# State-space heads: the decay rows go through device memory and are copied into all partitions, instead of being spread by a product

## The reference

```python
dt = softplus(dt_raw + dt_bias)              # (tokens, 2 directions, 32 heads)
a = -exp(a_log)
y_fwd = _ssd_scan(xs * dt[:, :, 0], dt[:, :, 0] * a[0], bm, cm)
y_bwd = flip(_ssd_scan(flip(xs * dt[:, :, 1]), flip(dt[:, :, 1] * a[1]), flip(bm), flip(cm)))
y = (y_fwd + y_bwd + d_skip * xs) * silu(z)
```

## Time and profile before

| what | value |
|---|---|
| median of 3 runs | 2443.31 us (2442.24 to 2443.97) |
| the profiled execution, its time | 2443.01 us |
| its span, from the first to the last instruction | 2441.1 us |
| PE busy | 2391.5 us (98%) |
| DVE busy | 1713.4 us (70%) |
| ACT busy | 1339.5 us (55%) |
| DMA engines, weight queue | 48.0% of 16 engines |
| granted clock of PE, mean of the span | 0.994 |

### The profile page before, as it was taken

The page is one execution under the profiler, slowest core; times in us unless marked ns, Lnnn a source line. Parts: engine busy times, 40 slices in busy tenths (PEclk is TensorE's granted clock), DMA queues, the critical chain, the costliest instruction groups (busy, mean ns, idle before and its releaser), DMA issues.

```text
span 2441.1 us, 48177 instructions
## 1 busy us (share of the span) xinstructions
PE 2391.5 (98%) x18842; PEld 2289.4 (94%) x18842; DVE 1713.4 (70%) x2517; ACT 1339.5 (55%) x2355; POOL 90.2 (4%) x101
## 2 busy tenths in 40 slices
PE   9999999999999999999999999999999999999998
PEld 8898999999899999999999997899999999789998
DVE  7788777777888867786766575676566657667665
ACT  6788655644678855563444445554444444555443
POOL 0000000000100000000100010010001001001000
PEclk9999999999999999999999999999999999999999
DMA  7454555455354455545455553345545544434553
GB/s 216 131 159 126 165 164 161 154 170 189 108 153 139 137 156 160 169 155 181 145 181 174 169 160 106 121 144 178 170 147 179 178 163 152 123 124 142 189 181 113
DMA packets 401046, 380.19 MB, mean 156 GB/s; under 512 B 28223, under 2 KB 397037, under 8 KB 400765
## 3 DMA queue, kind: packets, MB, share of 16 engines
q1 hardware_dynamic: 397821, 373.87, 48.0%
q10 hardware_dynamic: 3072, 4.20, 0.7%
HBM read 372.77 MB, written 1.05 MB: 153 GB/s over the span
## 4 chain that ended last, share of the span: by engine, by line
PE 79%; DVE 12%; ACT 3%; DVEq 3%; issue 1%; SPq 1%; DMA 1%; ACTq 0%
PE ps L583 22%; PE ps L585 21%; PE ps L584 21%; DVE scratch L1806 3%; DVE w_lo L1583 3%; DVEq L1805 2%; PE ps L805 2%; PE ps L836 1%; PE ps L837 1%; PE ps L838 1%; ACT scratch L1082 1%; ACT w_hi L1082 1%; PE ps L854 1%; PE ps L612 1%; PE ps L614 1%
## 5 line engine op out<-in xcount | busy, mean ns | idle before, releaser
L1583 DVE TENSOR_TENSOR w_lo<-raw,w_hi 128x1024 fp32r<-128x1024 f32 x664 | 812.0, 1229 | 423.2 <-ACT w_hi L1082 421.8
L583 PE MATMUL ps<-x_hi,w_hi 128*128 128x256 f32 (+1 forms) x3664 | 1056.4, 288 | 4.3 <-DVE w_lo L1583 1.6
L584 PE MATMUL ps<-x_lo,w_hi 128*128 128x256 f32 (+1 forms) x3664 | 1042.6, 285 | 0.0
L585 PE MATMUL ps<-x_hi,w_lo 128*128 128x256 f32 (+1 forms) x3664 | 1039.8, 284 | 0.0
L1082 ACT ACTIVATE w_hi<-raw 128x1024 fp32r<-128x1024 f32 x664 | 697.7, 1056 | 447.5 <-PE ps L585 370.6
L583 PEld LDWEIGHTS ps<-x_hi,w_hi 128*128 128x128 f32 x3664 | 690.8, 189 | 30.8 <-issue 25.3
L584 PEld LDWEIGHTS ps<-x_lo,w_hi 128*128 128x128 f32 x3664 | 692.2, 189 | 2.0
L585 PEld LDWEIGHTS ps<-x_hi,w_lo 128*128 128x128 f32 x3664 | 693.6, 189 | 0.0
L583 PE MATMUL ps<-big_r,w_hi 128*128 128x272 f32 (+1 forms) x832 | 238.9, 287 | 0.0
L585 PE MATMUL ps<-big_r,w_lo 128*128 128x272 f32 (+1 forms) x832 | 238.2, 286 | 0.0
L1082 ACT ACTIVATE scratch<-ps 128x256 f32<-128x256 f32 (+9 forms) x328 | 122.3, 384 | 154.9 <-PE ps L838 63.8
(11 more groups left out here) (302 smaller groups left out, 3063.1 us busy)
## 6 DMA issues: line engine op xcount, KB each, us to landing
raw<-in_w_in SPq DMA_DIRECT2D x184, 512.0 KB, 4.7
raw<-in_ffn_w_up SPq DMA_DIRECT2D x176, 512.0 KB, 4.3
raw<-in_ffn_w_down SPq DMA_DIRECT2D x64, 512.0 KB, 4.2
raw<-in_mix_w_in SPq DMA_DIRECT2D x64, 512.0 KB, 4.6
scratch<-in_w_in SPq DMA_DIRECT2D x40, 512.0 KB, 4.8
raw<-in_w_mem_kv SPq DMA_DIRECT2D x32, 512.0 KB, 4.8
raw<-in_w_br_ssd SPq DMA_DIRECT2D x32, 512.0 KB, 3.8
raw<-in_ffn_w_down SPq DMA_DIRECT2D x32, 384.0 KB, 3.3
```

The costliest lines, as they stand in the source:

```text
L583: mm(out, wh, xh, start=first, stop=False)
L584: mm(out, wh, xl, start=False, stop=False)
L585: return mm(out, wl, xh, start=False, stop=last)
L1583: tt(w_lo[:, p % PARTS, :, :], raw_at(slot_of(Q, p))[:, :, (p % 2) * P:(p % 2 + 1) * P], wh_f[:, p % PARTS, :, :], ALU.subtract).then_inc( ...
```

## The change

The spreading product is gone for all heads but the first two of each layer. ACT copies the 32 rows unrounded to `cum_rows`, writes them to device memory, and after `decays(j)` issues a transfer of the row of head j + 2 into all partitions of `even_row` or `odd_row`; `decays` reads that buffer. The first two heads of a layer are spread by a float32 product of the 32 rows (K = 32). `head_sel`, the remainder by DVE and the clearing by POOL are dropped.

```diff
-        cum_rows = nc.alloc_sbuf_tensor_at("cum_rows", [P, 2 * SEQ], F32R, offset=big_at + 4 * 7168)
+        cum_rows = nc.alloc_sbuf_tensor_at("cum_rows", [P, 2 * SEQ], F32, offset=big_at + 4 * 7168)
+        even_row = nc.alloc_sbuf_tensor_at("even_row", [P, 2 * SEQ], F32, offset=big_at + 4 * 7680)
...
+        odd_row = sb("odd_row", [P, 2 * SEQ])
+        rows_dram = nc.dram_tensor("cum_rows_dram", (DEPTH, SSD_HEADS, 2 * SEQ), F32, kind="Internal").ap()
...
                         cumulate()
+                        pe.wait_ge(S["row_ready"], l + 1)
                         pe.wait_ge(S["cum_ready"], l + 1)
-                        pe.wait_ge(S["row_ready"], l + 1)
-                        pe.wait_ge(S["rows_cleared"], l + 1)
-
-                    def spread_rows(j):
-                        if j >= 2:
-                            pe.wait_ge(S["expo_ready"], G * 8 + j - 1)
-                        h = g * HEADS_PER_GROUP + j
-                        sel = head_sel[:, h:h + 1].to_broadcast([P, P])
-                        mm(ps[2 + j % 2][:, :], sel, cum_rows[:, :], start=True, stop=True).then_inc(S["bc_done"], 1)
+                        for h in range(2):
+                            mm(ps[2 + h][:, :], const[0:SSD_HEADS, K_ID + h:K_ID + h + 1].to_broadcast([SSD_HEADS, P]), cum_rows[0:SSD_HEADS, :],
+                               start=True, stop=True).then_inc(S["first_rows"], 1)
...
-                    spread_rows(0)
-                    spread_rows(1)
                     for j in range(HEADS_PER_GROUP):
                         if j < 7 and (g or j >= 1):
                             proj(Q, T, 9 + j, 9 + j, x1)
-                        if j + 2 < HEADS_PER_GROUP:
-                            spread_rows(j + 2)
                         if j % 2 == 1:
                             head_pair(j // 2)
...
+                    def fetch_row(h):
+
+                        act.wait_ge(rows_out_done, 16 * (l + 1))
+                        act.wait_ge(S["expo_ready"], l * SSD_HEADS + h - 1)
+                        act.dma_start((even_row, odd_row)[h % 2][:, :], rows_dram[l, h].unsqueeze(0).to_broadcast([P, 2 * SEQ])).then_inc(head_row_in[h % 2], 16)
...
                         act.wait_ge(S["row_done"], l + 1)
-                        copy(cum_rows[0:SSD_HEADS, :], ps[3][0:SSD_HEADS, :]).then_inc(S["row_hi"], 1)
+                        copy(cum_rows[0:SSD_HEADS, :], ps[3][0:SSD_HEADS, :]).then_inc(S["row_ready"], 1)
+                        act.wait_ge(S["row_ready"], l + 1)
+                        act.dma_start(rows_dram[l], cum_rows[0:SSD_HEADS, :]).then_inc(rows_out_done, 16)
                         copy(cum_tok[:, :, :].rearrange("p t h -> p (t h)"), ps[2][:, 0:2 * 64]).then_inc(S["cum_ready"], 1)
...
-                        act.wait_ge(S["bc_done"], G * 8 + j + 1)
+                        if g == 0 and j < 2:
+                            act.wait_ge(S["first_rows"], 2 * l + j + 1)
+                            row = ps[2 + j]
+                        else:
+                            act.wait_ge(head_row_in[j % 2], 16 * (G * 4 + j // 2 - l))
+                            row = (even_row, odd_row)[j % 2]
                         for d, t, to, of in cuts:
                             at = d * SSD_HEADS + g * HEADS_PER_GROUP + j
-                            m = fn(expo[:, j % 2, to], ps[2 + j % 2][:, of], ACT.Relu, scale=-1.0, bias=cum_tok[:, t, at:at + 1])
+                            m = fn(expo[:, j % 2, to], row[:, of], ACT.Relu, scale=-1.0, bias=cum_tok[:, t, at:at + 1])
                         m.then_inc(S["expo_ready"], 1)
                         act.drain()
                         if j >= 4:
                             act.wait_ge(S["y_done"], G * 8 + j - 3)
                         fn(decay[:, j % 4, :], expo[:, j % 2, :], ACT.Exp, scale=-1.0).then_inc(S["decay_ready"], 1)
+                        if g * HEADS_PER_GROUP + j + 2 < SSD_HEADS:
+                            fetch_row(g * HEADS_PER_GROUP + j + 2)
...
-                    if g == 0:
-                        v.wait_ge(S["row_hi"], l + 1)
-                        tt(cum_rows[SSD_HEADS:2 * SSD_HEADS, :], ps[3][0:SSD_HEADS, :], cum_rows[0:SSD_HEADS, :].bitcast(F32),
-                           ALU.subtract).then_inc(S["row_ready"], 1)
```

More of the change, by code:

```diff
@@ L205, in build @@
         cum_tok = sb("cum_tok", [P, 2, 64])
-        head_sel = sb("head_sel", [P, SSD_HEADS], F32R)
+        odd_row = sb("odd_row", [P, 2 * SEQ])
+        rows_dram = nc.dram_tensor("cum_rows_dram", (DEPTH, SSD_HEADS, 2 * SEQ), F32, kind="Internal").ap()
         norm_bias = sb("norm_bias", [P, KT])
@@ L338, in build @@
         rot_in = [sem("q_rotated_in"), sem("k_rotated_in")]
+        head_row_in = [sem("even_head_row_in"), sem("odd_head_row_in")]
+        rows_out_done = sem("cum_rows_written")
         wr = [sem(f"weights_in{i}") for i in range(RAW + 1)]
@@ L345, in build @@
         params_in = sem("params_in")
-        names = ("idle_ready skip_ready mem_turned mem_ready x_turned xT_ready rows_turned rows_free late_turned late_free dt_hi_ready dt_lo_ready x_hi_ready mem_hi_ready rope_ready x_ready dt_done dt_pre dt_exp a_ready row_done row_hi row_ready cum_ready sel_ready rows_cleared first_tap conv_acc "
-                 "conv_tanh conv_ready xs_turned xdt_ready cb_done bc_done expo_ready decay_ready w_ready y_done "
+        names = ("idle_ready skip_ready mem_turned mem_ready x_turned xT_ready rows_turned rows_free late_turned late_free dt_hi_ready dt_lo_ready x_hi_ready mem_hi_ready rope_ready x_ready dt_done dt_pre dt_exp a_ready row_done row_ready first_rows cum_ready first_tap conv_acc "
+                 "conv_tanh conv_ready xs_turned xdt_ready cb_done expo_ready decay_ready w_ready y_done "
                  "y_gated y_squared sq_added ssq_done ssd_sum ssd_rs ssd_ready "
@@ L540, in _ @@
             with pool.Fori(0, DEPTH) as l:
-                pool.drain()
-                pool.memset(cum_rows[2 * SSD_HEADS:P, :].bitcast(F32), 0.0).then_inc(S["rows_cleared"], 1)
                 pool.drain()
@@ L1170, in small_params @@
                 fn(neg_a[:, :, :], neg_a[:, :, :], ACT.Exp).then_inc(S["nega_exp"], 1)
-                copy(head_sel[2 * SSD_HEADS:P, :], const[2 * SSD_HEADS:P, K_ID:K_ID + SSD_HEADS])
-                for r in (0, SSD_HEADS):
-                    m = copy(head_sel[r:r + SSD_HEADS, :], const[r:r + SSD_HEADS, K_ID + r:K_ID + r + SSD_HEADS])
-                m.then_inc(S["sel_ready"], 1)
                 act.wait_ge(S["lam_dot"], 1)
```

## The result

The changed kernel takes 2450.78 us in the median of 10 runs (2447.59 to 2452.88), the kernel before, timed beside it, 2442.96 us (2439.78 to 2445.82, 10 runs). The ratio is 1.0030, 95% interval 1.0022 to 1.0039: slower by 7.8 us. The forecast was "no change" (2444.0), and the time lies 6.8 us above it. The range of 2434 to 2457 held the time, but by the width that the rivals gave it: of the cases named, the late rows (2452) come nearest. The profiled execution took 2449.17 us, with a span of 2447.3.

What follows compares the result with a forecast made beforehand. DVE was taken to bound a group up to pair 0, then PE, with ACT taking over after the change. ACT's added costs less PE's gains summed to +0.7 us: 2443.7, or 2444.0 as median; range 2434 to 2457.

Steps and rivals of the forecast that it cites:

- the late rows: Rival: fetches take 5.0 us, ACT's Relu of head 2 waits; 7.6 us more, 2452; chance 0.20.
- What bounds a group: DVE limits up to pair 0, then PE over tiles 11 to 15; 57.8 us from pair 0 to pair 0.
- the bound of 58.5: Group 1 to group 2, pair 0 to pair 0: a length over 58.5 us would prove the prediction wrong.
- The bound of 17.6 us for all products: PE's stream: most the removal could bring, 64 products, half at 0.23 and half at 0.32 us.
- PE's half: Second half of a group, from pair 0: PE limits; removing products of heads 4 to 7 saves 1.1 us a group.
- SBUF reads: ACT's Relu reading the row from SBUF instead of PSUM: 0.09 us a head, 0.7 us a group.
- The issue: ACT issuing the fetch behind an Exp: 0.1 us a head, 0.8 us a group, mostly overlapped.
- slack of 1.2: ACT's waits for PE's tiles in the second half of group 1, 1.2 us in total; group 2 alike.
- The sum, +0.7 us in all: Whole kernel: group 0 +0.4 and +1.3, groups 1 and 2 +1.2, group 3 of both layers -2.2 us.
- The first heads: Start of a layer: from ACT's copy to its first Relu 0.8 us later, with pair 0 queued behind ACT.
- The fetch in time: Rows land in 2.8 us at a layer's first heads, 3.5 to 4 in groups, against 4.2 available: nothing late.
- The clock: Rival: PE's wait ahead of pair 0 grows to 2 us, clock falls, 1.7 us lost each; 2448.6; chance 0.05.

Runs made afterwards that it cites:

- before_again: The kernel before, unchanged, executed a second time; 2443.84 us, ratio 0.9998.
- sbuf_read_only: Kernel before with all its products, but ACT's Relu of 60 heads reads a constant in SBUF; 2443.20 us, ratio 0.9999.
- first_four_kept: Kernel before without the spreading products of heads 4 to 7 of every group, those of heads 0 to 3 kept; 2440.12 us, ratio 0.9991.
- half_fetched: Against the kernel before: products stay for heads 0 to 3, rows of heads 4 to 7 fetched into three buffers; 2445.32 us, ratio 1.0009.
- products_gone: Kernel before without spreading products except each layer's first two heads, no transfers instead; 2449.72 us, ratio 1.0030; again 2449.54 us (one run).
- gone_and_sbuf: Kernel before without spreading products except each layer's first two, Relu reading a constant in SBUF, no transfers; 2450.12 us, ratio 1.0032.
- four_ahead: The changed kernel with four row buffers, rows fetched four heads ahead instead of two; 2446.97 us, ratio 1.0019 to the kernel before.
- last_four_kept: Kernel before without products of heads 0 to 3 (except each layer's heads 0 and 1), those of heads 4 to 7 kept; 2448.64 us, ratio 1.0025.
- after_filled: The changed kernel plus ten unread products in PE's wait ahead of pair 0 in groups 1 to 3; 2448.90 us, ratio 1.0018 to the kernel before.
- four_ahead_filled: four_ahead plus ten unread products in PE's wait ahead of pair 0 in groups 1 to 3; 2439.81 us, ratio 0.9988 to the kernel before.
- all_groups_filled: four_ahead_filled with the ten unread products in group 0 of both layers too; 2445.07 us, ratio 1.0004 to the kernel before.

## Why it came out so

Three views over all profiles settle the sizes. First, the waits ahead of pair 0 in groups 1 to 3, two layers, and what the clock did behind them. In the eight profiles with waits of 0 to 1.5 us (`before`, `before_again`, `sbuf_read_only`, `first_four_kept`, `half_fetched` and the three filled ones) there are 48 such places and no fall. In the six with waits of 2.0 to 2.4 us (the change, `products_gone` twice, `gone_and_sbuf`, `four_ahead`, `last_four_kept`) there are 35, and behind 16 of them the clock fell (1, 4, 5, 2, 3 and 1); one more, of 1.6 us in the change, had none. Group 0, at a layer's first heads, is left out of this, since the clock is low ahead of pair 0 there in many profiles; it has six waits of 2.07 to 2.96 us, four of them with a fall. What decides whether such a wait is followed by a fall, no run tells.

Second, where each kernel stands at pair 2 of the last group (850.80 us in the kernel before), and what is added from there to the end of the span:

| kernel | to that pair | the rest |
|---|---|---|
| the change | +5.5 | +0.7 |
| after_filled | +4.9 | +0.1 |
| four_ahead | +2.3 | +1.4 |
| four_ahead_filled | -2.9 | +0.5 |
| all_groups_filled | +1.3 | +2.6 |
| half_fetched | -4.0 | +3.7 |
| first_four_kept | -6.1 | +3.3 |
| last_four_kept | +2.5 | +1.9 |
| products_gone; again | +2.5; +1.3 | +4.3; +5.3 |
| gone_and_sbuf | -1.0 | +5.7 |
| sbuf_read_only; before_again | -0.1; +0.1 | +1.7; +0.4 |

Third, the six groups from pair 0 to pair 0, us:

| kernel | layer 0 | layer 1 |
|---|---|---|
| before | 57.75, 57.45, 57.42 | 57.77, 57.77, 57.79 |
| the change | 57.80, 58.45, 58.18 | 58.92, 61.00, 57.66 |
| four_ahead_filled | 57.61, 57.38, 57.03 | 58.71, 57.38, 57.03 |

The first of layer 1 has a fall of the clock in both of the lower rows. The change's six groups are 6.9 us longer than those of `four_ahead_filled`, and the idle time of ACT for late rows is 6.8 us. The two agree group by group too: in group 1 of layer 1, the longest, it is 3.6 us more with 3.4 of waiting. The fall at 744 us, in that group, adds nothing: from its pair 3 to the next pair 0 it is 38.0 us in both kernels. So for the change's own profile the account closes: the same work with rows in time and without falls in groups 1 to 3 -2.9, late rows +6.9, the fall behind pair 0 of the last group +1.6 (pair 0 to pair 1 8.93 instead of 7.34), the rest of the program +0.7. The sum is +6.3, the span is 6.2 longer. The median of the time is 7.8 above; how often the clock falls in the runs without a profile is not known.

Now the steps of the prediction.

*What bounds a group* was right. From pair 0 of group 1 to pair 0 of group 2 it is 58.45 us (57.8 foretold), in layer 1 61.0, over the bound of 58.5 beyond which the prediction called itself wrong. PE's busy time fell by 7.8 us and not by 15; among other things, products at the lower clock take longer, and the float32 products for the first two heads take 1.95 us a layer where two spreading products took 0.70. The bound of 17.6 us for all products was itself too high: 60 go, not 64, and of a group's eight three stand ahead of a pair, which makes 24 x 0.32 + 36 x 0.23 = 16.0; nothing else hangs on it. Products of heads 0 to 3 bought nothing (the wait ahead of pair 0 grew from 1.1 to 2.03, as foretold), those of heads 4 to 7 stand in PE's half. Their size was 0.9 us a group (two steps from 7.79 to 7.34), not 1.1.

*SBUF reads* were put at 0.09 us a head and cost 0.15 (1.48 against 1.33). *The issue* was put at 0.1 and costs 0. Together ACT pays 1.2 us a group, not 1.5, about its slack of 1.2. It takes back 0.5 us of PE's 0.9 (`gone_and_sbuf`), and with the rows in time a group comes out not 0.3 longer but up to 0.8 shorter. The sum, +0.7 us in all, measures -2.9 up to pair 2 of the last group and -2.4 over the span in `four_ahead_filled`, where the rows are in time and the wait is filled. The row of `rotate` was read for an issue of 0.61 us, four transfers of another form; this one takes 0.33.

*The first heads.* From ACT's copy to its first Relu it is 2.58 us (61.22 to 63.80) against 1.90, 0.7 later where 0.8 was forecast. But the copy itself starts 1.0 earlier, since the clock was low under PE's sums in the profile of before (two of their products took 1.06 us there, 0.62 here). And pair 0 of layer 0 did not hang on ACT, as the prediction had it: in the kernel before PE comes to it without a wait, from its own products. It starts at 69.41 instead of 70.56, not later.

*The fetch in time* is the step of the mechanism that failed: "I take 2.8 there and 3.5 to 4 in the groups: nothing late". The median landings are 5.0 and 4.2 us, up to 6.5, against a distance of 4.2 us. The bound of 5.0 from the earlier trace rows, set aside as one from the crowd of the start, was the better one. The Trainium skill's "DMA: Bandwidth & Descriptors", "Anatomy of one DMA", has its 2.0 us and 436 GB/s from transfers that GpSimd issued; the prediction carried them over to ACT's queue for its estimate of 2.6 us. The trace has 3.0 at the least, and the measurement decides. The rival of late rows was right in place (the Relu of head 2) and near in price (7.6 forecast, 6.9 measured), the latter partly by luck. At a layer's first heads it foretold 2.2 us each, and they were 0.6 and 0.5, landing in 3.2 and 3.1 us; in groups 1 and 2 it foretold 3.2 together and they were 4.0; and 1.8 came at the Relu of head 7 (in group 2 of layer 0 and group 1 of layer 1), which it did not name. Its chance of 0.20 was too low.

*The clock* had the rival's mechanism right (wait of 2 us, lower level behind it, 1.7 us a time; measured 1.5 to 1.6) and its chance too low. The Trainium skill's "TensorE: Matmul & The Clock Gate", Part 1, has idleness lower the clock; the trace agrees in this, with 16 falls behind 35 waits of 2 us. In the change it is the smaller of two losses. In `four_ahead` the three falls turn a gain into a loss within the first part; in `products_gone` the four do so together with a wait of PE of 1.9 us at about 285 us, with a fall behind it, that its second execution had at 0.3 us.

**What stays open.** Behind the first part no kernel differs from the one before, and yet 0 to 5.7 us are added there, the same in a second execution of the same kernel to within 1.0 us. The same happens between the groups of the two layers, where 285 us is such a place. The places are few: the starts of feed-forward parts (1218 us in the rows above; at 2249 us a wait of 1.5 us in `first_four_kept` and 1.4 in `half_fetched`, 0.6 before), and in `first_four_kept` a wait of PE of 1.6 us at about 872 us, where DVE stood 3.0 us waiting for `rotate`'s transfer, as in `last_four_kept` and `products_gone` at 285 us. Where such a wait could be followed, it led over DVE and ACT to a transfer that came in late against the engines. What sets that, no run here tells apart. It is why `products_gone` loses 6 us while its first part loses only 1.3 to 2.5, and why `first_four_kept` keeps 3 of its 6.1 us.

## What to carry to other kernels

Work that an engine has time for can still be holding something up: here four cheap products a group kept PE's wait at 1.1 us, and without them the clock fell in about half of the groups. Before taking work from a waiting TensorE, ask how long its wait becomes, and where it comes near the 2 us of this case, try filling; but measure each place, since filling the first group of each layer as well made the kernel 4.7 us slower. A transfer that replaces an operation of 0.3 us needs its distance measured against landings under the load of that stage (here 3.0 to 6.5 us for 256 KB), not against those of a quiet one; four buffers instead of two took all of the lateness away but 0.4 and 0.3 us at a layer's first heads. And what is won in one part may not reach the end: compare the place of one instruction behind the part and the span before calling it a gain.

## What the runs showed of the hardware

An issue of a transfer on ACT's queue took 0.33 us and began 0.08 us after the start of the Exp ahead of it, so under an instruction of 0.85 us it was free. Relu pieces with a pointer as bias took 0.50 us for 256 columns out of SBUF and 0.48 out of PSUM (0.39 and 0.36 for 128). The two writes of 64 KB by ACT to device memory landed in 3.74 and 4.04 us. And the clock came back under work: in `products_gone` the products step by 0.21 us from 185.9 on and by 0.12 again from 188.5 on, with PE busy throughout. A fall of the clock in the half of a group where DVE sets the pace cost nothing; behind pair 0, where PE sets it, 1.5 to 1.6 us.
